# A two-layer encoder trunk: a fourth 64-slot expert item, the last two items small, 4 KB packets, and the scatter ahead of the next item

## The reference

```python
D_MODEL, SEQ, D_FF_EXPERT, N_EXPERTS, TOP_K = 1024, 256, 2816, 8, 2

def swiglu(h, w_gate_up, w_down):
    g, u = jnp.split(h @ w_gate_up, 2, axis=-1)
    return (jax.nn.silu(g) * u) @ w_down

def moe(h, router, w_gate_up, w_down):
    xt = h.reshape(B * S, D)
    probs = jax.nn.softmax((xt @ router).astype(jnp.float32), axis=-1)
    top_p, top_i = lax.top_k(probs, TOP_K)
    top_p = top_p / jnp.sum(top_p, axis=-1, keepdims=True)
    gates = jnp.sum(jax.nn.one_hot(top_i, N_EXPERTS) * top_p[..., None], axis=1)
    y = jnp.zeros_like(xt)
    for e in range(N_EXPERTS):
        y = y + gates[:, e:e + 1] * swiglu(xt, w_gate_up[e], w_down[e])
    return y.reshape(B, S, D)
```

## Time and profile before

| | |
|---|---|
| time, median of 3 runs | 1203.26 us (1202.2 to 1205.78) |
| the profiled execution: its time, its span | 1204.16 us, 1202.4 us |
| mean granted clock of TensorE | 0.969 |
| PE matmul, weight load, DVE, ACT busy | 94%, 70%, 59%, 49% of the span |
| DMA over the span | 343.23 MB, 285 GB/s |
| transfers of expert weights | 352 + 176 of 512 KB, that is 8 items of 66 |

### The profile page before, as it was taken

The page is one execution under the profiler, slowest core; times in us unless marked ns, Lnnn a source line. Parts: engine busy times, 40 slices in busy tenths (PEclk is TensorE's granted clock), DMA queues, the critical chain, the costliest instruction groups (busy, mean ns, idle before and its releaser), DMA issues.

```text
span 1202.4 us, 15887 instructions
## 1 busy us (share of the span) xinstructions
PE 1127.3 (94%) x5499; PEld 845.2 (70%) x5499; DVE 703.8 (59%) x746; ACT 593.4 (49%) x627; POOL 14.0 (1%) x81
## 2 busy tenths in 40 slices
PE   7999999999999888999979999969999969999995
PEld 6867788888898776885337885337884337887884
DVE  6745555455654457983027973027973028978895
ACT  6444534334436536762026762126762126767773
POOL 1100000000000000000000000000000000000000
PEclk9879999999999979999989999989999989999998
DMA  9932456455455317998999999999999999999950
GB/s 354 313 105 84 162 176 205 179 175 205 148 179 169 106 35 241 363 366 299 390 397 387 391 396 366 392 396 387 392 395 349 392 396 387 393 394 336 379 206 35
DMA packets 166473, 343.23 MB, mean 285 GB/s; under 512 B 11869, under 2 KB 50826, under 8 KB 166410
## 3 DMA queue, kind: packets, MB, share of 16 engines
q1 hardware_dynamic: 166266, 341.93, 78.4%
q10 hardware_dynamic: 144, 0.52, 0.1%
HBM read 341.37 MB, written 1.05 MB: 285 GB/s over the span
## 4 chain that ended last, share of the span: by engine, by line
PE 78%; SPq 7%; DMA 5%; DVE 5%; issue 3%; ACT 2%; DVEq 0%; POOL 0%; POOLq 0%; ACTq 0%
PE ps L1396 22%; PE ps L1397 21%; PE ps L1398 21%; PE ps L1401 11%; SPq L327 7%; DMA raw<-moe_w_gate_up_dram 4%; DMA raw<-moe_w_down_dram 1%; DVE wlo L887 1%; PE ps L1710 1%; ACT whi L494 1%; DVE h L1069 1%; PE ps L1411 1%; DVE wlo L876 0%; DVE xlo L1112 0%; DVE h L1141 0%
## 5 line engine op out<-in xcount | busy, mean ns | idle before, releaser
L494 ACT ACTIVATE whi<-raw 128x2048 fp32r<-128x2048 f32 (+1 forms) x228 | 399.2, 1754 | 324.6 <-PE ps L1398 263.8
L887 DVE TENSOR_TENSOR wlo<-raw,whi 128x2048 fp32r<-128x2048 f32 x184 | 420.1, 2290 | 213.0 <-ACT whi L494 212.2
L1396 PE MATMUL ps<-whi,xhi 128*128 128x512 f32 (+1 forms) x744 | 298.3, 401 | 39.8 <-DVE xlo L1112 25.4
L1397 PE MATMUL ps<-whi,xlo 128*128 128x512 f32 (+1 forms) x744 | 291.9, 392 | 0.0
L1398 PE MATMUL ps<-wlo,xhi 128*128 128x512 f32 (+1 forms) x744 | 291.8, 392 | 0.0
L1396 PEld LDWEIGHTS ps<-whi,xhi 128*128 128x128 f32 x744 | 142.5, 192 | 77.1 <-DVE xlo L1112 28.1
L1398 PEld LDWEIGHTS ps<-wlo,xhi 128*128 128x128 f32 x744 | 142.5, 192 | 29.4
L1397 PEld LDWEIGHTS ps<-whi,xlo 128*128 128x128 f32 x744 | 142.8, 192 | 26.7
L1396 PE MATMUL ps<-whi,hhi 128*128 128x512 f32 x308 | 123.2, 400 | 0.0
L1397 PE MATMUL ps<-whi,hlo 128*128 128x512 f32 x308 | 121.7, 395 | 0.0
L1398 PE MATMUL ps<-wlo,hhi 128*128 128x512 f32 x308 | 121.6, 395 | 0.0
(11 more groups left out here) (282 smaller groups left out, 967.0 us busy)
## 6 DMA issues: line engine op xcount, KB each, us to landing
raw<-moe_w_gate_up_dram SPq DMA_DIRECT2D x352, 512.0 KB, 9.6
raw<-moe_w_down_dram SPq DMA_DIRECT2D x176, 512.0 KB, 11.2
raw<-ffn_w_gate_up_dram SPq DMA_DIRECT2D x44, 512.0 KB, 4.9
raw<-ffn_w_down_dram SPq DMA_DIRECT2D x22, 512.0 KB, 3.7
raw<-kv_shared_w_dram SPq DMA_DIRECT2D x16, 512.0 KB, 4.6
raw<-mla_w_o_dram SPq DMA_DIRECT2D x8, 512.0 KB, 14.3
raw<-sb_w_q_dram SPq DMA_DIRECT2D x8, 512.0 KB, 3.8
raw<-sb_w_o_dram SPq DMA_DIRECT2D x8, 512.0 KB, 3.7
```

What stands on the lines that cost most here:

```text
L494: return nc.scalar.activation(o, i, ACT.Copy, scale=scale)
L887: V.tensor_tensor(wlo[:, s, :].rearrange("p a w -> p (a w)"), raw[:, (hh // 2) % RAW, :], whi[:, s, :].bitcast(F32).rearrange("p a w -> p ...
L1396: pe.matmul(o, a_hi, b_hi, start=start, stop=False, skip_group_check=True)
L1397: pe.matmul(o, a_lo, b_hi, start=False, stop=False, skip_group_check=True)
```

## The change

1. `NS` goes from 3 to 4, and `ORDER` gives big, small, big, small, big, big, (overflow items, if any), small, small. The loop over pairs runs twice (`PAIRS`), then come the big items, then two small ones.
2. The units of gate and up are cut otherwise. Units 0 to 7 hold one row block k each, with 1024 gate and 1024 up columns; units 8 to 15 the same for the next 1024 columns; units 16 to 21 the last 768 columns (`segments`). A row in a transfer is 4096 bytes in the first 16 units, and 3072, 2048 or 1024 bytes in the last six, which have 3, 4 and 3 transfers. A big item so has PSUM sums of two groups open at a time: groups 0 and 1 end with unit 7, groups 2 and 3 with unit 15, groups 4 and 5 with unit 21, in banks given by `sub_bank`. The half-width matmuls of the last group are twice as many at 256 columns. A small item has 4 groups.
3. All transposes go to one bank (`TR_BANK`). Those of groups 0 and 1 stand after units 9 and 10, of 2 and 3 after 17 and 18, of 4 and 5 after the down units 1 and 2 (counted from 0), and each waits for `h_lo` of the group before it.
4. The scatter stands straight behind the last down unit. Behind it PE does units 0 and 1 of the next item, no longer four; the transposes of the selection matrix come after unit 8. ACT copies them to `selN`, and POOL multiplies `selN` by itself into `selT` (entries are 0 or 1).

```diff
-MW = 512
-MG = 6
-MU = (0, 4, 8, 12, 16, 20, 22)
+GU = 22
 SMALL = 64
-NS = 3
+NS = 4
 NB = N_EXP - NS
-ORDER = (0, 1, 4, 2, 5, 3, 6, 7)
+PAIRS = 2
 OVF = 5
-ITEMS = N_EXP + OVF + 1
+FIRST_OVF = 6
+LATE = FIRST_OVF + OVF
+ITEMS = LATE + 2
+ORDER = (0, 1, 5, 2, 6, 7) + OVF * (-1,) + (3, 4)
+SUB = 6
+
+def sub_width(j):
+    return 512 if j < SUB - 1 else 256
+
+def sub_bank(j):
+
+    return (0, 2, 4, 0, 2, 7)[j]
+
...
+TR_BANK = 6
+
+def segments(x):
+
+    if x < 16:
+        return [(a * 1024, x % 8, a, x // 8 * 1024, 1024) for a in range(2)]
+    k, c = (x - 16) // 3 * 4, 2048
+    return (
+        [(0, k, 0, c, 768), (768, k, 1, c, 768), (1536, k + 1, 0, c, 512)],
+        [(0, k + 1, 0, c + 512, 256), (256, k + 1, 1, c, 768), (1024, k + 2, 0, c, 768), (1792, k + 2, 1, c + 512, 256)],
+        [(0, k + 2, 1, c, 512), (512, k + 3, 0, c, 768), (1280, k + 3, 1, c, 768)])[(x - 16) % 3]
+
                 u = U_MOE + x
-                if x < MU[MG]:
...
+                if x < GU:
+                    for place, k, a, c, n in segments(x):
+                        sp_eng.dma_start(raw[:, u % RAW, place:place + n], w_gu[k * P:(k + 1) * P, a * FF + c:a * FF + c + n]
+                                         ).then_inc(landed[u % RAW], 16)
                 else:
...
-            with sp_eng.Fori(NS + 1, final + 1) as i:
-                big_loads(i, at(i + NS), lambda x: after_big(x, i - 1))
+            with sp_eng.Fori(PAIRS + 1, final + 1) as i:
+                big_loads(i, at(i + PAIRS), lambda x: after_big(x, i - 1))
+            small_loads(PAIRS, at(LATE), lambda x: after_big(x, final))
+            small_loads(PAIRS + 1, at(LATE + 1), lambda x: after_small(x, PAIRS))
...
+            def scatter_weights(g):
+
+                pool.wait_ge(selN_ready, g + 1)
+                nc.gpsimd.tensor_tensor(selT[:, :], selN[:, :].bitcast(F32), selN[:, :].bitcast(F32), ALU.mult).then_inc(selT_ready, 1)
+
+            scatter_weights(0)
+            pool.wait_ge(items_ready, 2)
+            final = pool.value_load(final_i[0:1, 0:1], min_val=NB - 1, max_val=NB - 1 + OVF)
+            with pool.Fori(0, final + NS) as g:
+                scatter_weights(g + 1)
...
+            def big(i, g, following):
...
+                for x in range(2, FU):
+                    if x in (7, 15, 21):
+                        silu({7: 0, 15: 2, 21: 4}[x])
+                    if x == 9:
+                        transposed(g)
+                    if x in (10, 11, 18, 19, 24, 25):
+                        high({10: 0, 11: 1, 18: 2, 19: 3, 24: 4, 25: 5}[x])
+                    if x == FU - 1:
                         act.wait_ge(used, i * FH + H_MOE + FH)
                         for m in range(2):
-                            copy(xhi[:, 4 * m:4 * m + 4, P:SEQ], ps[:, 6 + m, :].rearrange("p (a s) -> p a s", a=4)).then_inc(y_hi, 1)
...
+            def small(p, g, following):
...
+                if following == "big":
+                    for x in range(2):
+                        split_high_unit(H_MOE + 2 * x, p + 1, g + 1)
+                    gathered_high(p + 1, g + 1)
+                    split_high_unit(H_MOE + 2 * 2, p + 1, g + 1)
+                if following == "small":
+                    gathered_small(g + 1)
+                copy(ys[:, :], ps[:, 4, :]).then_inc(ys_ready, 1)
...
+                for x in range(2, FU):
+                    if x in (7, 15, 21):
+                        gate({7: 0, 15: 2, 21: 4}[x])
+                    if x in (10, 11, 18, 19, 24, 25):
+                        low({10: 0, 11: 1, 18: 2, 19: 3, 24: 4, 25: 5}[x])
+                    if x == 14:
+                        item_gates(g, row)
+                        choose(g + 1, next_row, following)
+                    if x == FU - 1:
...
+                    if x + 3 < FU or following == "big":
...
+            def big_unit(x, i, g):
+
+                hh = H_MOE + 2 * x
+                pe.wait_ge(lo_made, i * FH + hh + 2)
+                whi_x, wlo_x = unit_split(whi, x), unit_split(wlo, x)
+                if x < 16:
+                    k = x % 8
+                    if x < 8:
+                        pe.wait_ge(xe_lo, i * KD + k + 1)
+                    if x == 8:
+                        pe.wait_ge(h_ready[4], g * 4 + 4)
+                    for n in range(2):
+                        j = 2 * (x // 8) + n
+                        if k == 0 and j == 3:
+                            pe.wait_ge(gated[2], i * SUB + 1)
+                        for a in range(2):
+                            w = slice(a * 1024 + n * 512, a * 1024 + (n + 1) * 512)
+                            last = mm3(ps[:, sub_bank(j) + a, :], xhi[:, k, 0:P], xlo[:, k, 0:P],
+                                       whi_x[:, w], wlo_x[:, w], k == 0, k == KD - 1)
+                        if k == KD - 1 and n == 0:
+                            last.then_inc(even_done, 1)
...
+            def begin(following, i, g):
+
+                for x in range(2):
+                    if following == "big":
+                        big_unit(x, i, g)
...
+                for x in range(2, GU):
+                    big_unit(x, i, g)
+                    if x == 8:
+                        selection(g)
+                    if x == 9:
+                        pe.wait_ge(selN_ready, g + 1)
+                    if x in (9, 10, 17, 18):
+                        transposes({9: 0, 10: 1, 17: 2, 18: 3}[x])
+                for d in range(FU - GU):
+                    hh = H_MOE + 2 * (GU + d)
...
+                    if d in (1, 2):
+                        transposes(d + 3)
+                    if d == 5:
+                        pe.wait_ge(h_lo[2], i * SUB + SUB)
                         gather(g + 1)
+                gathered_out(following, next_i)
                 pe.wait_ge(y_lo, i * 2 + 2)
+                pe.wait_ge(selT_ready, g + 1)
                 for c in range(TC):
                     for n in range(2):
                         o = ps[:, 4 + 2 * c + n, :].rearrange("p (a s) -> p a s", a=4)
                         w = selT[:, c * P:(c + 1) * P]
                         mm(o, w, xhi[:, 4 * n:4 * n + 4, P:SEQ], True, False)
                         mm(o, w, xlo[:, 4 * n:4 * n + 4, P:SEQ], False, True).then_inc(scattered, 1)
+                begin(following, next_i, g + 1)
+
...
-            with pe.Fori(NS, final) as i:
-                big(i, i + NS, "big", i + 1)
-            big(final, final + NS, None)
+            with pe.Fori(PAIRS, final) as i:
+                big(i, i + PAIRS, "big", i + 1)
+            big(final, final + PAIRS, "small", PAIRS)
+            small(PAIRS, final + PAIRS + 1, "small", PAIRS + 1)
+            small(PAIRS + 1, final + PAIRS + 2, None, None)
```

More of the change, by code:

```diff
@@ L274, in moe_landed, with unit_raw, unit_split @@
         def moe_landed(x, g):
-            u = U_MOE + x
-            return landed[u % RAW], g * LANDS + 32 * (u // RAW + 1)
-        def gate_up(x):
-            w = MW if x < MU[MG - 1] else MW // 2
-            return raw[:, (U_MOE + x) % RAW, :].rearrange("p (k a f) -> p k a f", a=2, f=w)
+            slot = (U_MOE + x) % RAW
+            of_slot = [n for n in range(FU) if (U_MOE + n) % RAW == slot]
+            a_unit = 32 * sum(u % RAW == slot for u in range(U_MOE))
+            within = 16 * sum(transfers(n) for n in of_slot if n <= x)
+            return landed[slot], g * (16 * sum(transfers(n) for n in of_slot)) + a_unit + within
+        def unit_raw(x):
+            return raw[:, (U_MOE + x) % RAW, :]
+        def unit_split(t, x):
+            r = (H_MOE + 2 * x) % RING
+            return t[:, r:r + 2, :].rearrange("p a w -> p (a w)")
         @block.sync
@@ L756, in small @@
-                split_high_unit(H_MOE + 2 * 2, p + 1, g + 1)
+                    act.wait_ge(small_tr, p * SMALL_GROUPS + j + 1)
+                    w = SMALL_WIDTH[j]
+                    copy(hT[:, SMALL_FIRST[j]:SMALL_FIRST[j] + w], ps[:, TR_BANK, 0:w]).then_inc(hT_ready, 1)
+                silu(0)
+                transposed(g)
+                hidden(0)
+                silu(1)
+                hidden(1)
+                silu(2)
+                silu(3)
+                hidden(2)
+                hidden(3)
@@ L1157, in low @@
                                     ehi[:, chunks, :].bitcast(F32).rearrange("p a s -> p (a s)"), ALU.subtract).then_inc(h_lo[2], 1)
-                for j in range(1, MG):
-                    gate(j - 1)
-                    if j >= 2:
-                        low(j - 2)
-                    for x in range(MU[j], MU[j + 1]):
-                        split_low_unit(H_MOE + RING + 2 * x, i)
-                    if j == 3:
-                        item_gates(g)
-                        if following is not None:
-                            choose(g + 1, following)
@@ L1169, in big @@
-                gate(MG - 1)
-                low(MG - 2)
-                for d in range(FU - MU[MG]):
-                    x = MU[MG] + d + RING // 2
```

(40 more changed lines are left out.)

399 lines of the change are left out of this document (175 added, 224 removed).

## The result

The changed kernel takes **1240.15 us** (median of 4 runs, 1237.01 to 1243.63), against 1204.52 for the kernel before on the same chip: ratio **1.030** (95% interval 1.0255 to 1.034). The forecast was 1221 us, with a range of 1184 to 1234: the sign was right, but 19 us are missing, and the range doesn't hold the time. The profiled execution has a span of 1241.9 us; the forecast's sum for it was 1220.2.

A forecast was written before the change was run, and what follows sets the result against it. Big items were taken as PE-bound, small ones as load-bound. First small start 565.0, two small items 152.2, big items 113.5, 114.6 and 111.5, and last two 163.4 gave 1220.2 us span, forecast 1221, range 1184 to 1234.

The forecast's parts named there:

- What bounds the kernel: Kernel before: big items (103.3 us) bound by PE with DMA full beside it, small ones (75.0 us) by loads.
- Part 2, the waits: Inside big items: PE waits 2.3 us before transposes three times and 1.3 us for the gated product, 8.2 us an item.
- the transposes don't wait: Rival for big items: ACT and DVE slack hides the transpose waits, without 4 x 8.2 us; 1188 us, chance 0.17.
- Part 2, the step that failed: Big items: the new waits were counted at 8.2 us an item, with no term for half clock behind them.
- the long gap: Small to big: PE idles 8.47 us before its first product in the kernel before, with clock 0.50 granted there.
- Part 3, the scatter: End of items: +2.0 us idle per big item, +3.1 before another big one; scatter 1.9 us, ending 8.2 after landing.
- The second landing: Small items: unit 1 of the next big item lands 67.9 us after the start, from 8.6 + 23 x 2.58.
- Part 1, packets: Loads: longer rows bring a unit to 2.58 us in the mean, 0.10 less, counting only where loads bound.
- the larger packets bring nothing: Rival for the loads: row length is of no account, 10 us more; 1231 us, chance 0.10.
- Part 4 and the end: Eight items, four big and four small; the last two small ones take 163.4 us to the kernel's end.
- the rival with half clock there: Last item: TensorE at half clock needs 3.5 us a unit where 2.58 come in, +31; 1252 us, chance 0.04.
- POOL's product: Between unit 9 and the scatter: the product of selN costs nothing; bounds 0 and 2 us, hidden at either end.

The follow-up runs named there:

- the filled gap in the kernel before: The kernel before plus 34 unread matmuls in TensorE's 9.07 us gap at each of three changes from small to big item: 1202.9 us, ratio 1.0000.
- filling the waits: The changed kernel plus nine unread matmuls ahead of each of three waits for hlo and the wait for y in a big item: 1223.4 us.
- the run that kept its clock: The changed kernel with the first 16 units of an item loaded in rows of 2048 bytes in place of 4096: 1239.8 us.
- the kernel with alternating items and filled gaps: The changed kernel with two transpose banks, scatter behind two units, big and small items by turns, and 40 unread matmuls per small-to-big gap: 1174.1 us.

## Why the prediction was wrong in size

- **What bounds the kernel**: half right. "Big items are bound by PE with DMA full beside it" was true of one item. Over a pair the loads were the bound, as the filled gap in the kernel before shows. This didn't spoil the sum, since the changed kernel left the loads idle in its big items.
- **Part 2, the waits**: right. 8.2 us forecast; by starts 2.36 + 2.22 + 2.31 in place of 0.23 each (0.12 for the second), and 1.37 in place of 0.23 for the gated product: 7.4 us. Taking those for `hlo` away brought 37 us; the rival "the transposes don't wait" falls. The sign, too, is no luck: without these waits and the one for `y` the kernel is 1.7% faster than before.
- **Part 2, the step that failed:** a wait was priced at its length. The forecast named half clock twice, for the long gap and for the last item, and wrote "small items wait at full clock until the long gap". It didn't ask what waits of 2.3 us do in big items: the clock behind them was a term put at nothing without a reason. The trace shows half clock behind 13 of 16 waits, 1.7 us of work each, and filling the waits gives 17 us. That this is nearly the missing 19 is in part chance: the big items lie only 12.9 us above the forecast, and with the clock held 4.5 below it, 3 of these because the waits were put at 8.2 us; another 8.2 us are missing in the small items and 3.0 at the end.
- **Part 3, the scatter**: 2.0 us forecast after a big item, 2.0 in the waits; 3.1 forecast where a big item follows, 3.7 there. At small to big the forecast let the scatter run at full clock 8 us into a gap, though the earlier trace rows show 0.50 behind that gap: it took 3.8 us, not 1.9. That, and a second landing at 69.7 us and not at 67.9, make 79.8 and 80.6 us of the 76.1.
- **The second landing**: the lag was taken from the kernel before, whose loads ran on at the small item's start. Now all slots are full then and no transfer starts for 7 us (563.5 to 570.5), while PE does the scatter and its first unit; then the rate is as forecast (406 GB/s, 2.58 us a unit):

```profile
563.50:570.50 7.00, 6.58 (x22) 2.96 (x24) 3.09 (x5) 0.00 (x0) 0.00 (x0) 0.76 0.00 0
570.50:577.50 7.00, 7.00 (x34) 2.25 (x32) 0.00 (x0) 0.00 (x0) 0.00 (x0) 1.00 0.96 320
577.50:636.20 58.70, 54.55 (x345) 24.41 (x341) 3.31 (x9) 5.91 (x11) 0.69 (x1) 1.00 1.03 406
```

- **Part 1, packets**: right. The mean of 2.58 us a unit was right, and so was its reason: with the rows cut back to 2048 bytes the transfers came at 387 GB/s, with 4096 at 410, in the same part of two kernels that differ in nothing else, and with DVE and ACT nearly idle. The rival "the larger packets bring nothing" is wrong on the mechanism; that its 1231 us lie nearer to the measured 1240 is chance. What the larger packets are worth in time stays open: the two pairs of kernels with both row lengths differ by 0.4 and 0.1 us. The Trainium skill (DMA: Bandwidth & Descriptors, where 436 GB/s comes from) puts the bound of such loads at about 358 GB/s a core. This core moved 387 and 410, so the measurement decides.
- **Part 4 and the end**: eight items, as forecast. The two last took 166.4 us, not 163.4; their transfers came at 393 GB/s in the mean, and TensorE ran at full clock in them nearly to the end, against the rival with half clock there. A fourth small item is worth 32 us.
- **The sum by stretches**, measured less forecast: first big item +3.9 (119.8 against 115.9, the 103.8 of before and 12.1), small +3.7, big +4.8, small +4.5, big +0.7, big +3.5, end +3.0. Together 24.1; the expert part also began 2.4 us earlier than in the kernel before (446.7 against 449.1), which leaves 21.7 of span.
- **POOL's product** cost nothing that a wait shows. It was not tested by itself.

## What to carry to other kernels

Where TensorE is the bound, a wait of some 2 us can cost more than its length: about half as much again came from the clock here. So price the stretch behind a new wait at both clock levels, and widen the range by it. Read a bound over the whole period of the loop, and not over one item of it; a resource that is full for the whole period takes back what another gains, and one that has become idle hides nothing. Read the rate of a row length from a stretch in which all packets have that length, and don't take a rate for a time: here 6% of rate moved the kernel's time by less than its noise.

## What was not expected of the hardware

- Half clock can follow waits of 2.2 to 2.4 us, and not always: behind 13 of the 16 waits for `hlo` and `y` in the changed kernel's profile (one of them 4.1 us from start to start, the others 2.2 to 2.4), behind 3 of the same 16 in the run on rows of 2048 bytes.
- Matmuls whose result nobody reads held the clock (0.99 to 1.00 in the big items with filled waits, 0.94 to 0.97 without). Where TensorE would have idled anyway they cost nothing that shows: 114.4 us for the first big item with filled waits, and 114.4 without them in the run that kept its clock.
- In the kernels with more code in the loop of pairs, TensorE stops where the loop returns. Of the kernel with alternating items and filled gaps:

```profile
816.13 1.45 PE L1445 MATMUL ps<-ys,selT 64*128 64x512 f32 x6
819.77 0.49 PE L1440 MATMUL ps<-whi,xhi 128*128 128x512 f32 x1 [2.19 <-issue]
```

From start to start of the last scatter matmul and the next product it is 2.8 us, and 0.5 where the loop is left. The kernel before has 0.5 at both. In the changed kernel the gap stands at 652 us, between the second unit and the third; the row names `wlo`, but the split of the third unit was done at 644.75:

```profile
652.05 0.39 PE L1450 MATMUL ps<-wlo,xhi 128*128 128x512 f32 x1
654.69 0.49 PE L1448 MATMUL ps<-whi,xhi 128*128 128x512 f32 x1 [2.26 <-DVE wlo L947]
```

The trace of the kernel before has 31 packets of 16 KB in the instruction queue q8, none of them between 616 and 1006 us. The changed kernel has 48, some of them in the second pass of the loop and two at 652 and 658 us. The filled gap in the kernel before brought 41 and a gap of 2.9 us at the first return.

```profile
q8 instruction: 48, 0.79, 0.3%
```

That code loading causes the gap, about 2 us of the second big item's +4.8, is read from the traces and was not tested.
